# Four plain up blocks instead of eight in each MLP layer, with two more pairs in seven half products

## What is computed

```python
def squared_relu_mlp(h, w_up, w_down):
    u = jax.nn.relu(h @ w_up)
    return (u * u) @ w_down

for layer in range(DEPTH):                     # DEPTH = 2
    ...                                        # the mixer of the layer
    h = h + squared_relu_mlp(rms_norm(h, g_mlp[layer]), w_mlp_up[layer], w_mlp_down[layer])
```

## Time and profile before

| what | value |
|---|---|
| three runs, median (lowest to highest) | 2468.08 us (2466.75 to 2468.46) |
| profiled execution, its span from first to last instruction | 2466.2 us |
| TensorE busy | 2453.5 us (99%) |
| VectorE busy | 1518.7 us (62%) |
| ScalarE busy | 1062.5 us (43%) |
| TensorE's share of the chain that ended last | 94% |
| plain up blocks of the first MLP layer, from its first to its last | 266.7 to 314.6 us |

### The profile page before, as it was taken

One profiled execution on the slowest core, in us unless ns is written; L12 is line 12 of the kernel. 1 busy time (PEld: TensorE's weight loads), 2 busy tenths in 40 slices (PEclk: granted clock), 3 DMA queues, 4 the chain that ended last, 5 costly groups with the idle time before them and its releaser, 6 DMA issues.

```text
span 2466.2 us, 33484 instructions
## 1 busy us (share of the span) xinstructions
PE 2453.5 (99%) x12408; PEld 2056.6 (83%) x12408; DVE 1518.7 (62%) x2084; ACT 1062.5 (43%) x1477; POOL 121.9 (5%) x107
## 2 busy tenths in 40 slices
PE   9999999999999999999999999999999999999999
PEld 7888789998888888789988888888787778888887
DVE  6777756666766765756656545545868846544343
ACT  3676535545334343535536333224465453323222
POOL 2000100001000000100002000002000001000000
PEclk9999999999999999999999999999999999999999
DMA  4111345542222222245532232233222222232223
GB/s 141 57 52 60 130 132 141 146 128 86 94 82 72 82 89 84 95 147 152 163 119 63 99 102 94 94 101 109 80 70 71 74 69 94 95 101 94 95 101 111
DMA packets 86459, 244.67 MB, mean 99 GB/s; under 512 B 13392, under 2 KB 23888, under 8 KB 86224
## 3 DMA queue, kind: packets, MB, share of 16 engines
q1 hardware_dynamic: 78656, 228.54, 27.6%
q0 software_dynamic: 3456, 12.58, 3.0%
q10 hardware_dynamic: 4240, 2.10, 0.3%
HBM read 241.09 MB, written 2.10 MB: 99 GB/s over the span
## 4 chain that ended last, share of the span: by engine, by line
PE 94%; DVE 3%; issue 1%; POOL 1%; ACT 0%; DMA 0%; SPq 0%; ACTq 0%; DVEq 0%; POOLq 0%
PE ps L2511 44%; PE ps L2516 21%; PE ps L2854 7%; PE ps L2867 3%; PE ps L2858 3%; PE ps L3193 2%; PE ps L2580 2%; PE ps L2936 1%; PE ps L2564 1%; PE ps L2735 1%; PE ps L2692 1%; PE ps L2711 1%; PE ps L2676 1%; PE ps L2923 1%; PE ps L2698 1%
## 5 line engine op out<-in xcount | busy, mean ns | idle before, releaser
L724 ACT ACTIVATE w_hi<-raw 128x1024 fp32r<-128x1024 f32 x358 | 379.7, 1061 | 1009.8 <-PE ps L2516 928.1
L2511 PE MATMUL ps<-x_hi,w_hi 128*128 128x512 f32 x1552 | 614.2, 396 | 4.3 <-DVE u_act L1856 4.3
L2511 PE MATMUL ps<-x_lo,w_hi 128*128 128x512 f32 x1552 | 606.3, 391 | 0.0
L1479 DVE TENSOR_TENSOR w_lo<-raw,w_hi 128x1024 fp32r<-128x1024 f32 x358 | 440.7, 1231 | 104.8 <-ACT w_hi L724 104.5
L2516 PE MATMUL ps<-x_hi,w_lo 128*128 128x512 f32 x1552 | 383.4, 389 | 0.0
L2511 PEld LDWEIGHTS ps<-x_hi,w_hi 128*128 128x128 f32 x1552 | 292.7, 189 | 70.4 <-issue 9.1
L2511 PEld LDWEIGHTS ps<-x_lo,w_hi 128*128 128x128 f32 x1552 | 292.7, 189 | 60.9 <-issue 1.7
L2516 PEld LDWEIGHTS ps<-x_hi,w_lo 128*128 128x128 f32 x1552 | 291.3, 188 | 60.6
L2511 PE MATMUL ps<-u_hi,w_hi 128*128 128x512 f32 x730 | 284.5, 390 | 0.0
L2511 PE MATMUL ps<-u_lo,w_hi 128*128 128x512 f32 x730 | 284.1, 389 | 0.0
L2516 PE MATMUL ps<-u_hi,w_lo 128*128 128x512 f32 x730 | 180.9, 389 | 0.0
(11 more groups left out here) (454 smaller groups left out, 3758.8 us busy)
## 6 DMA issues: line engine op xcount, KB each, us to landing
raw<-in_stream SPq DMA_DIRECT2D x365, 512.0 KB, 3.3
forms<-in_stream SPq DMA_DIRECT2D x72, 256.0 KB, 4.3
forms<-in_stream SPq DMA_DIRECT2D x24, 512.0 KB, 5.0
forms<-in_stream POOLq DMA_DIRECT2D x24, 512.0 KB, 6.4
x_tok<-in_x SPq DMA_DIRECT2D x4, 512.0 KB, 7.9
out_x<-xn ACTq DMA_DIRECT2D x7, 256.0 KB, 2.3
tab_ret<-in_tables_ret SPq DMA_DIRECT2D x1, 1536.0 KB, 6.6
raw<-in_stream SPq DMA_DIRECT2D x3, 256.0 KB, 3.2
```

Source lines behind the costliest of these rows:

```text
L724: nc.scalar.activation(w_hi[:, slot(n)], raw[:, slot(n)], ACT.Copy).then_inc(hi_done, 1)
L1479: nc.vector.tensor_tensor(w_lo[:, slot(n)], raw[:, slot(n)], w_hi[:, slot(n)].bitcast(F32), ALU.subtract).then_inc(lo_done, 1)
L2511: nc.tensor.matmul(ps[:, gemm_bank(n)], w_hi[:, s, k], x(k), start=(k == 0 and i == 0), stop=False)
```

## The change

```diff
-UP_DENSE = 8
+UP_DENSE = 4
 MLP_DENSE = UP_DENSE + DC * len(MLP_GROUPS)
 UP_PAIRS = (HIDDEN // P - UP_DENSE) // 2
```

## The result

The changed kernel takes 2478.42 us (median of 5 runs, 2477.80 to 2479.28) against 2468.08 us (2466.75 to 2468.49, 5 runs) for the kernel before. The medians differ by 10.3 us; the ratio is 1.0044, 95% interval 1.0032 to 1.0056, so the kernel is slower by 0.44%. The profiled span is 2477.5 us, 11.3 us longer than before; the profiled execution was the slowest of the five (2479.28 us). The prediction was 2476.7 us, in a range of 2472 to 2483 us.

What follows compares the result with a forecast made beforehand. The prediction took PE (TensorE) as the bound. To the 2466.2 us span it added a loss of 4.3 us in each of two layers, giving 2474.8, and with the median 1.9 above the span forecast 2476.7 us, range 2472 to 2483.

Steps and rivals of the forecast that it cites:

- The bound: Whole kernel: PE is 94% of the last chain; its only sizeable wait is 4.3 us for DVE's relu, one piece per layer.
- The wait for the high part: After the fourth plain block PE idles 8.3 us, instead of 2.3, for ACT's high part of the first form.
- The low part's place: On DVE, the first form's low part starts 1.94 us after chunk 3's, giving PE a second short wait.
- how long the clock stays low: After PE's idle stretch ahead of the units, the clock stays at the lower level for 3.3 us.
- The bound in the text: If the clock stayed low through the second unit too: 1.3 us a layer more, 2.6 in all.
- The half matmul at the low clock: In the first unit on PE, a half matmul at the lower clock takes 0.227 us, scaled from full matmuls.
- Units at 1.44 us after that: The first group's thirteen units after the first take 1.44 us each on PE, 18.72 us.
- DMA hidden: Added-up forms land some 9.5 us ahead of DVE's sum; the first down block's load has 4.2 us in hand.
- The pair's saving: On PE, a pair replacing two plain blocks saves 0.80 us: 1.60 a layer, 3.2 for four pairs.
- Rival 1: Units start without waiting after the plain blocks: 11.2 us gained, 2457 us; chance 5%.
- Rival 2: DVE's low part comes 2 to 3 us earlier beside an idle PE: 2470.7 to 2472.7 us; chance 7%.
- Rival 3: The first down block's load lands late, holding ACT's split 3.9 us: 2484.5 us; chance 8%.

Runs made afterwards that it cites:

- e2: Changed kernel with the loads of the first two pairs' forms let go one plain block later: 2478.82 us.
- e10: e9 with the next group's first parts made behind the first group's last results on ACT and DVE, and the second weight split one unit earlier: 2458.56 us.
- e6: Changed kernel with the MLP norms' reciprocal and square of the inverse moved to the end of the first group's pairs on DVE: 2472.93 us.
- e8: Changed kernel with the inverse later as in e6 and the first pair's parts ahead of the third and fourth plain blocks' results on DVE and ACT: 2471.03 us.
- e9: e8 with ACT copying the first unit's product right behind that unit, and the first two down blocks' weights split during the units: 2477.60 us.
- e1: Changed kernel with 30 idle matmuls on PE between the fourth plain block and the first unit of each MLP layer: 2477.36 us.
- e3: Changed kernel with the reciprocal of the two MLP norms on DVE replaced by a copy of the same tile: 2472.95 us.
- e7: Kernel before, with the reciprocal in two halves and the square of the inverse moved behind later plain blocks on DVE, all work kept: 2460.34 us.

## Why the prediction came out

- **The bound** (PE, and in it the wait at the seam of plain blocks and the rest): right. The other groups are as before and the loss sits in the two seams.
- **The wait for the high part**: 8.3 us forecast; by the same reckoning, from block 3's end, 297.38 - 289.10 = 8.28 us in layer 0 (the row's 8.12 counts from the end of the last matmul, in both layers). PE goes on at 297.38, forecast 297.20. Taking DVE's and ACT's times over unchanged was right to 0.2 us: chunk 3's low part begins at 296.74 instead of 296.57.
- **The low part's place**: forecast 1.94 us behind the low part of chunk 3, measured 298.68 - 296.74 = 1.94. The second short wait, for DVE's low part, is there too: the four matmuls on it start 0.41 us after the one before them, where the others start 0.21 apart. The first unit ends where the next begins, at 300.44, forecast 300.26.
- **The mis-sized term: how long the clock stays low.** The step took 3.3 us from the earlier trace rows, over by the end of the first unit. It lasted from 297.4 to about 302 in layer 0, 4.6 us, and from 1050.0 to 1056.3 in layer 1, 6.3 us. In layer 0 the second unit takes 302.58 - 300.44 = 2.14 us instead of 1.44, so 0.7 us more; in layer 1 the second takes 1055.63 - 1053.07 = 2.56 us and the third 1057.41 - 1055.63 = 1.78, so 1.46 us more, and the reckoning from block 3's end gives 31.52 us against a forecast 30.07, 1.45 more. Together 2.1 us: a loss of 10.7 against 8.6 forecast, out of the 2.7 us by which the profiled span lies above its forecast (2477.5 against 2474.8); the median lies 1.7 us above. The bound in the text (the second unit too at the low clock, 1.3 us a layer, 2.6 in all) held for the sum but not for layer 1, where the clock rose only in the third unit.
- **The half matmul at the low clock**: I scaled 0.227 us; the eight start 0.213 us apart (297.73 to 299.01 is 1.28 us for six). The Trainium skill, "TensorE: Matmul & The Clock Gate", section "Back-to-back issue gap", gives 256 columns / 1.2 GHz = 0.213 us there, and the trace agrees. The difference weighs 0.2 us a unit at most.
- **Units at 1.44 us after that**: right, ten from 302.58 to 316.98 in layer 0.
- **DMA hidden**: right. Forms were issued at 272.49 and the added-up ones at 280.37, and e2 puts the loads a block later at next to no cost.

```profile
272.49 0.34 SPq L646 DMA_DIRECT2D forms<-in_stream  x1
...
280.37 1.01 POOL L2469 DMA_DIRECT2D forms<-in_stream  x1 [9.94 <-DMA forms<-in_stream]
```

- **The pair's saving**, 0.80 us: the steady units bear it out, but in the changed kernel it can't be seen by itself. In e10 half of it is left.
- **Rival 1** (units start without waiting, 2457 us) did not happen to this change, but its size was near: with the work put in another order it is 2458.6 us. I gave as its condition that DVE shed 3.9 us; e6 and e8 show that this does not do alone (in e6 4.0 us left DVE's queue and PE still waits 5.3), since ACT, a copy out of PSUM and SP's queue each held PE in turn. **Rival 2** (half the loss) would have needed DVE faster beside an idle PE: its steps take as long as before and keep their places to 0.2 us. **Rival 3** (a load late too) is excluded for this kernel by e2, where a block's delay costs half a us; it did strike e9, where the load was late by SP's queue.

## What to carry to other kernels

A product with fewer multiplications needs more of the engines that prepare it, and it needs that before its first matmul: ahead of shortening a cover, add up what the helping engine still owes at the moment when the cover ends, from its own timeline. Here the change saved 3.2 us of matmuls and added 12 us to PE's waits (16.2 instead of 4.3), before the lower clock behind them; the remedy was to move what nobody needed yet (an inverse, weight splits, the next group's parts) behind what PE needed now, and each such move had to be followed through ACT's order, PSUM banks and SP's queue before the gain arrived. When a wait's releaser is given as "issue", look on the other engines for what ended just before it.

## What the runs showed of the hardware

After the same idle stretch of 8.12 us the lower clock lasted 4.6 us in one layer and 6.3 in the other of one execution, and 3.3 us after the 2.15 us of the earlier trace rows: a duration read once is not a constant. The prediction's one reading was short in both layers. In e1, with PE busy through most of the wait, the clock stayed up in one layer and fell for 3.5 us in the other. So a wait should be priced with a range for what follows it.

One reciprocal on DVE takes 3.35 us where a subtraction of the same 128 x 512 takes 0.69, 4.9 times as long. The Trainium skill's "VectorE: DVE Perf Modes", section "First, the fixed hardware budget", says that it is done by an iterative division with eight repeats. It gives no time for it; the ratio here is 4.9, and e3 and e7 show what it costs where it stands ahead of PE.
